# One SiLU gate block of the second layer: exponential on ScalarE, the rest on VectorE one head later, and its store moved with it

## The reference: what is computed

```
q, k, v, qi, ki, wi, z = jnp.split(h @ w_in, DSA_SPLITS, axis=-1)
...
o = dsa_attention(q, k, v, qi, ki, wi, top_k).reshape(B, S, DSA_WIDTH)
return (o * jax.nn.silu(z)) @ w_out
```

## Time and profile before

| | |
|---|---|
| median of 3 runs | 1307.49 us (1307.03 to 1308.07) |
| time of the profiled execution | 1307.25 us |
| its span in the trace | 1305.4 us |
| PE busy | 1285.7 us, 98% of the span |
| DVE busy | 784.2 us, 60% |
| ACT busy | 571.0 us, 44% |
| POOL busy | 530.1 us, 41% |
| PE's share of the chain that ended last | 93% |

### The profile page before, as it was taken

One profiled execution on the slowest core, in us unless ns is written; L12 is line 12 of the kernel. 1 busy time (PEld: TensorE's weight loads), 2 busy tenths in 40 slices (PEclk: granted clock), 3 DMA queues, 4 the chain that ended last, 5 costly groups with the idle time before them and its releaser, 6 DMA issues.

```text
span 1305.4 us, 19013 instructions
## 1 busy us (share of the span) xinstructions
PE 1285.7 (98%) x6866; PEld 1101.9 (84%) x6866; DVE 784.2 (60%) x1547; ACT 571.0 (44%) x1142; POOL 530.1 (41%) x721
## 2 busy tenths in 40 slices
PE   9999999999999999999999999999999999999997
PEld 8878889999998888888887888888889998888885
DVE  7623746555656435335467899867887777154334
ACT  8312235454554213124235576677566664033122
POOL 1852024555544744334420433331356654654301
PEclk9999999999999999999999999999999999999999
DMA  6232341211210531224231333232322112522122
GB/s 209 68 105 81 119 132 49 66 57 50 73 33 25 186 101 51 84 64 138 89 89 34 96 98 104 89 122 85 106 82 93 59 32 81 158 82 72 53 65 89
DMA packets 89900, 113.22 MB, mean 87 GB/s; under 512 B 9936, under 2 KB 52176, under 8 KB 89808
## 3 DMA queue, kind: packets, MB, share of 16 engines
q1 hardware_dynamic: 89808, 112.00, 27.8%
HBM read 81.04 MB, written 27.79 MB: 83 GB/s over the span
## 4 chain that ended last, share of the span: by engine, by line
PE 93%; DVE 2%; POOL 2%; ACT 2%; issue 1%; POOLq 0%; DVEq 0%; ACTq 0%
PE psum L1828 27%; PE psum L1830 27%; PE psum L1829 27%; PE psum L2037 5%; PE psum L2021 3%; PE psum L2005 2%; PE psum L1868 2%; PE psum L1879 1%; POOL ring_lo L1238 1%; PE psum L1913 1%; ACT act_hi L1279 0%; PE psum L1849 0%; ACT p L1432 0%; POOL ring_hi L1235 0%; DVE xr L1685 0%
## 5 line engine op out<-in xcount | busy, mean ns | idle before, releaser
L1828 PE MATMUL psum<-ring_hi,act_lo 128*128 128x512 f32 x816 | 322.1, 395 | 0.7 <-DVE act_lo L1816 0.7
L1830 PE MATMUL psum<-ring_hi,act_hi 128*128 128x512 f32 x816 | 318.7, 391 | 0.0
L1829 PE MATMUL psum<-ring_lo,act_hi 128*128 128x512 f32 x816 | 318.5, 390 | 0.0
L1235 POOL CAST ring_hi<-raw 128x512 fp32r<-128x512 f32 x128 | 82.8, 647 | 337.5 <-DMA raw<-in_dsa_w_in 178.8
L1466 DVE TENSOR_TENSOR act_lo<-psum,act_hi 128x512 fp32r<-128x512 f32 (+3 forms) x276 | 155.8, 593 | 63.7 <-ACT act_hi L1279 37.3
L1238 POOL TENSOR_TENSOR ring_lo<-raw,ring_hi 128x512 fp32r<-128x512 f32 x128 | 183.7, 1435 | 10.3
L1828 PEld LDWEIGHTS psum<-ring_hi,act_lo 128*128 128x128 f32 x816 | 153.8, 188 | 32.7 <-DVE act_lo L1816 1.4
L1830 PEld LDWEIGHTS psum<-ring_hi,act_hi 128*128 128x128 f32 x816 | 153.6, 188 | 32.3
L1829 PEld LDWEIGHTS psum<-ring_lo,act_hi 128*128 128x128 f32 x816 | 153.9, 189 | 30.9
L1279 ACT ACTIVATE act_hi<-psum 128x512 fp32r<-128x512 f32 (+1 forms) x244 | 114.8, 511 | 144.0 <-PE psum L2037 73.6
L1249 POOL TENSOR_TENSOR small<-small 128x1 f32<-128x1 f32 x128 | 70.9, 554 | 167.2 <-ACT p L1432 110.6
(11 more groups left out here) (268 smaller groups left out, 2435.7 us busy)
## 6 DMA issues: line engine op xcount, KB each, us to landing
raw<-in_dsa_w_in SPq DMA_DIRECT2D x48, 256.0 KB, 3.1
gz<-z_scratch SPq DMA_DIRECT2D x16, 512.0 KB, 3.4
raw<-in_ple_w_gate SPq DMA_DIRECT2D x32, 256.0 KB, 3.1
raw<-in_mla_w_in SPq DMA_DIRECT2D x19, 256.0 KB, 2.9
xr<-in_x_t SPq DMA_DIRECT2D x16, 256.0 KB, 6.5
z_scratch<-gz SPq DMA_DIRECT2D x16, 256.0 KB, 2.0
raw<-in_mla_w_out SPq DMA_DIRECT2D x16, 256.0 KB, 3.4
p<-in_x SPq DMA_DIRECT2D x16, 256.0 KB, 3.1
```

The costliest lines, as they stand in the source:

```text
L1235: last = nc.gpsimd.tensor_copy(dst, src[:, c0:c0 + cols])
L1828: nc.tensor.matmul(dst, lhs(1), rhs(0), start=start, stop=False)
L1829: nc.tensor.matmul(dst, lhs(0), rhs(1), start=False, stop=False)
L1830: return nc.tensor.matmul(dst, lhs(0), rhs(0), start=False, stop=stop)
```

## The change

The last gate block of layer 1 is no longer put through SiLU by ACT. ACT copies the bank to `xr[:, 59 * P:63 * P]` and writes exp(-z) of the same bank to `xr[:, 36 * P:40 * P]`, with the same wait for `found`. A new step `z_last`, put in the plan behind the fifth query block of head 1 (`i == 4 and h == 1`), lets DVE do 1 + exp(-z), its reciprocal, and the product with z, and lets SP store the result then. The first `z_load`s no longer wait for that store.

```diff
+                last = base and job == 7
+                s = proj(lay, i, job, ["zs"], {"zs": 1} if last else {"zs": 1, "z_st%d" % slot: 1}, slot=slot, base=base,
+                         side_read=now["found"], ring="B" if last else "A")
+                last_gate.append(s.after["zs"])
...
+            if i == 4 and h == 1:
+                add("z_last", {"z_last": 1, "z_st1": 1}, ready=last_gate[-1])
...
+        def late_gate():
+
+            return xr[:, 59 * P:63 * P], xr[:, 36 * P:40 * P]
...
+                elif k == "z_last":
+                    sp.wait_ge(sem["z_last"], 1)
+                    sp.dma_start(z_dram[1][D - P:D, CW:2 * CW], late_gate()[0]).then_inc(sem["z_st1"], 16)
+                elif k == "proj" and n["name"] == "z" and not is_last_gate(s):
...
-                            if n["base"] and n["job"] == 7:
+                            if is_last_gate(s):
+
+                                gate, grown = late_gate()
                                 act_e.wait_ge(sem["found"], n["side_read"])
+                                nc.scalar.activation(gate, bank(b), ACT.Copy)
+                                nc.scalar.activation(grown, bank(b), ACT.Exp, scale=-1.0).then_inc(sem["zs"], 1)
+                                continue
...
+                elif k == "z_last":
+
+                    gate, grown = late_gate()
+                    dve.wait_ge(sem["zs"], n["ready"])
+                    linked(nc.vector.tensor_scalar(grown, grown, 1.0, None, ALU.add))
+                    linked(nc.vector.reciprocal(grown, grown))
+                    nc.vector.tensor_tensor(gate, gate, grown, ALU.mult).then_inc(sem["z_last"], 1)
```

More of the change, by code:

```diff
@@ L94 @@
               "xadd", "sg", "pp", "relu", "sc", "nb", "ex", "pn", "og", "stage", "trig",
-              "consts", "ones", "strip", "xsq", "xacc", "tok_ms", "tok_rs", "dg_hi", "dg_lo", "rb", "zr", "vcopy", "found", "thr", "sgn", "widx", "w_hi", "w0", "fk", "tally", "cand", "pool_chain", "dve_chain", "fin"]
+              "consts", "ones", "strip", "xsq", "xacc", "tok_ms", "tok_rs", "dg_hi", "dg_lo", "rb", "zr", "vcopy", "found", "thr", "sgn", "widx", "w_hi", "w0", "fk", "z_last", "tally", "cand", "pool_chain", "dve_chain", "fin"]
 class Step:
@@ L256, in plan @@
     gate_free = {}
+    last_gate = []
     def z_chunk(lay, i, base, prefetch=True, extra=None):
@@ L265, in z_chunk @@
             else:
-                proj(lay, i, job, ["zs"], {"zs": 1, "z_st%d" % slot: 1}, slot=slot, base=base,
-                     side_read=now["found"], ring="B" if base and job == 7 else "A")
+                last = base and job == 7
+                s = proj(lay, i, job, ["zs"], {"zs": 1} if last else {"zs": 1, "z_st%d" % slot: 1}, slot=slot, base=base,
+                         side_read=now["found"], ring="B" if last else "A")
+                last_gate.append(s.after["zs"])
                 gate_free[slot] = now["z_st%d" % slot]
@@ L990, in qi_parts, with is_last_gate @@
             return xr[:, (6 + slot) * D + CW:(7 + slot) * D], (xr[:, 5 * D + CW:6 * D], p0[:, CW:2 * CW])[slot]
+        def is_last_gate(s):
+            return s.n["lay"] == 1 and s.n["base"] and s.n["job"] == 7
+        def late_gate():
+            return xr[:, 59 * P:63 * P], xr[:, 36 * P:40 * P]
         def gate_rows(s):
-            if s.n["lay"] == 1 and s.n["base"] and s.n["job"] == 7:
-                return xr[:, 59 * P:63 * P]
             return (gz, p0)[s.n["lay"]][:, s.n["slot"] * CW:(s.n["slot"] + 1) * CW]
@@ L1136, in _ @@
                     sp.dma_start(cs[:], cs_dram).then_inc(sem["cs_ld"], 16)
-                elif k == "proj" and n["name"] == "z":
+                elif k == "z_last":
+                    sp.wait_ge(sem["z_last"], 1)
+                    sp.dma_start(z_dram[1][D - P:D, CW:2 * CW], late_gate()[0]).then_inc(sem["z_st1"], 16)
+                elif k == "proj" and n["name"] == "z" and not is_last_gate(s):
                     sp.wait_ge(sem["zs"], s.after["zs"])
@@ L1371, in _ @@
                             act_e.wait_ge(sem["a_full"], s.after["a_full"])
-                            if n["base"] and n["job"] == 7:
+                            if is_last_gate(s):
+                                gate, grown = late_gate()
                                 act_e.wait_ge(sem["found"], n["side_read"])
-                            elif s.before["z_st%d" % slot]:
+                                nc.scalar.activation(gate, bank(b), ACT.Copy)
+                                nc.scalar.activation(grown, bank(b), ACT.Exp, scale=-1.0).then_inc(sem["zs"], 1)
+                                continue
+                            if s.before["z_st%d" % slot]:
                                 act_e.wait_ge(sem["z_st%d" % slot], s.before["z_st%d" % slot])
```

## The result

The changed kernel takes 1310.80 us (median of 9 runs, 1309.50 to 1312.13), the kernel before in the same comparison 1307.25 us (9 runs, 1306.61 to 1308.24). The ratio is 1.0027, 95% interval 1.0018 to 1.0036: 3.6 us slower, where 1310.6 was forecast.

A forecast was written before the change was run, and what follows sets the result against it. PE, busy 98% of the span, was taken to bound the kernel. A cost of 4.3 us from the delayed DVE reduce, less a gain of 1.2, gave 3.1 us more: 1310.6 us, own range 1309.6 to 1311.6, whole range 1306.5 to 1311.9.

The forecast's parts named there:

- What bounds the kernel, and that the shift stays: PE is busy 98% of the span; a shift PE has by 1020 us it keeps to the end.
- The two loads: ACT near the 16th gate block: the loads for SiLU and back to Exp go, 2.57 us; block 7's copies 1.4 us earlier.
- The gain on PE: PE's three gaps behind the loads in head 0 shrink: 1.2 us gained, bounds 0.5 to 1.7.
- the first gap: PE's 0.43 us gap before 942.47, waiting for DVE's low parts of block 6: it loses 0.15 us.
- The third gap: PE's 0.55 us gap before 950.87, waiting for a row from a reduce queued on DVE: shrinks by 0.35.
- SP's queue: Store at 941.14 moves away, first gate load at 943.22 may go some 3 us earlier: worth nothing.
- The reciprocal, R: Duration of DVE's reciprocal over 512 columns in head 1, estimated at 4.45 us; the term that decides.
- eight passes: Forecast case for DVE's reciprocal, three bits a pass: 4.45 us, net 3.1 us slower; chance 0.56 without a clock fall.
- two to six passes: Rival: DVE's reciprocal takes 1.2 to 3.4 us, net -0.2 to +2.0, time 1308.5; chance 0.10.
- The cost on PE, D - 1.25: D, the delay of DVE's reduce at 969.32 in head 1, is 5.55 us; 1.25 is absorbed, so PE loses 4.3.
- The clock: Rival: PE's idleness in head 1 drops the granted clock to 1.2 GHz, up to 3 us more, 1312 to 1313; chance 0.06.
- the forecast case: Reciprocal of eight passes on DVE in head 1, clock not falling: 3.1 us slower, 1310.6; chance 0.56.

The follow-up runs named there:

- the experiment that keeps the loads: Kernel before, SiLU, both table loads and store kept, with only the three DVE instructions added on spare columns in head 1: 5.15 us above the kernel before.
- The experiment one head later: Changed kernel with step z_last at the same query block of head 2 instead of head 1: 1312.6 us over five runs.
- the two fillings: Changed kernel with extra PE matmuls in head 1's waits: nine unread ones (median 1309.65 us), or block 2's scores done five times over (1308.45 to 1311.34 us).
- the four quarters: Changed kernel with the three DVE instructions cut into four parts of 128 columns, behind query blocks 6 and 4 of heads 1 and 2: 1308.81 us.
- the first filling: Changed kernel with 9 unread 512-column matmuls on PE ahead of the score block of query block 3 in head 1: median 1309.65 us.

## Why the prediction was right, and where only by the sum

**What bounds the kernel, and that the shift stays:** right. 3.05 us are lost by head 3, and the 295 us behind it are unchanged to 0.1.

**The two loads:** right. They went, nothing took their place, and ACT's copies of block 7 came 1.7 us sooner; 1.4 was forecast. The further 1.38 us of drain for each switch, which the Trainium skill's page "ScalarE: Activation LUTs", section "What ACT_TABLE_LOAD costs", gives, did not show in the experiment that keeps the loads either: its load at 942.57 ends at 943.85, and the Exp behind it starts at 943.86.

**The gain on PE:** 1.2 forecast, 1.40 measured in head 0, 1.36 to 1.44 in head 3 without the cost. It lies within the bounds of 0.5 to 1.7, but its parts were sized wrongly. Counted from the load, PE passes the first gap 0.26 us sooner (0.15 was forecast), is 1.13 ahead behind the second (0.86), and 1.31 after a short delay that no row shows as a gap. The third gap gave only 0.09 more, where 0.35 was forecast, and still stands at 0.52 us:

```profile
949.96 0.77 PE L2063 MATMUL psum<-ident,cs 128*128 128x128 f32 x5 [0.52 <-POOL cs L1264]
```

**SP's queue:** right. The first gate load moved from 943.22 to 939.66, the store went out at 972.97, and without the reciprocal no loss was left.

**The reciprocal, R:** the term that decides was mis-sized. I took eight passes, 4.45 us; it is 3.35, by 6.25 ns per column against 1.06 for one pass. That is the price of six passes; no run shows that it works in passes, or how many bits one finds. It sits in the rival "two to six passes", which would have given at most 2.0 us net.

**The cost on PE, D - 1.25:** with the clock held the count is +1.59, so the cost is 1.59 + 1.36 = 2.95 of D = 4.45. What vanishes is 1.5 us, not 1.25. The path was the right one: in the change itself the lateness shrinks from 3.05 us at the reduce of block 5 to 1.62 at that of block 3, and ACT's idle 1.13 us ahead of the copies of `T` of block 4 are gone. The experiment one head later supports that this slack belongs to the place: with the clock held it ends about 1.3 us later than the 1309.1 that the two fillings show in such executions. That rests on one execution; that PE has no wait of its own in head 2, and the costs of the four quarters, speak for it too.

**The clock:** I gave its fall 6 in 100, on top of eight passes. By their mean granted clocks it fell in all nine executions of the change. The price is 3.05 - 1.59 = 1.5 us in the profiled ones, and 2.5 us between the means of the two groups of the first filling; why it is more there is open, since no execution of the slower group was profiled. So two errors met: 1.1 us too much in R, and 1.5 us left out for the clock, with 0.25 more absorbed and 0.2 more gained. The forecast of 3.1 and the 3.05 of this stage agree by luck, since these cancel, and not because the sum was right in its parts. By its own terms with the true R the forecast case would have been 2.0 us, within 0.2%.

What stays open is what makes the clock fall in one execution and not in the next of the same kernel. It stayed up through a wait of 2.59 us in one profiled execution, and fell at the end of one of 2.33, and just behind one of 1.67, in others.

## What to carry to other kernels

Taking a table switch off ACT was worth here what it closed of PE's gaps behind it, 1.4 us of the 2.6 that ACT no longer spends on loads. What is put on another engine for it has to fit into the slack of the very place where it goes: the same 1.43 us on DVE cost PE 0.2 us at one place and 1.4 at another. That slack is read from the waits there, not from the engine's busy share. Before a division is moved to DVE, look for a function in the table set that is already loaded which needs none: with Tanh the same idea was worth 1.7 us instead of costing 3.6. And a stall of PE has a second price, the slower clock behind it, which varied between executions: compare each run's granted clock before a difference of 1 or 2 us is explained.

## What the hardware showed that I had not expected

- DVE's reciprocal in f32 took 953, 1753 and 3353 ns for 128, 256 and 512 columns: 6.25 ns per column and 153 ns of start. The one of 128 columns:

```profile
L1791 DVE RECIPROCAL xr<-xr 128x128 f32<-128x128 f32 x4 | 3.8, 953 | 0.1
```

- TensorE's granted clock fell to 1.2 GHz at the end of a wait of only 2.33 us, and in the kernel with half the reciprocal 0.6 us behind one of 1.67 us, and stayed there for about 6.8 and 3.4 us although PE was at work again. At the end of the kernel before, it fell only some 3.2 us after PE's last matmul.
